# Turning attention probabilities by transposing DMAs in place of TensorE transposes, in a four-mixer hybrid block

## The chip, the cores and the metric

The kernel runs on one core of a Trainium2 chip. A core has five engines with a program each: TensorE (PE) multiplies matrices into PSUM banks, VectorE (DVE) and ScalarE (ACT) work on SBUF and PSUM, GpSimd (POOL) on SBUF, and SyncE (SP) issues DMAs. Each engine works its own list of instructions in order and waits on semaphores. The metric is the device time of one execution in microseconds; lower is better.

## The reference

One layer of a decoder over 2048 tokens of width 1024. The input is normalised and projected; four groups of heads mix over the sequence; the result is gated, projected by `w_out`, normalised and added to the input. What matters of it, cut:

```python
h = _rmsnorm(x, pre_norm[l])
(a_q, a_k, a_v, sb_q, sb_k, sb_v, f_q, f_k, f_v, f_logit, m_q, gate) = jnp.split(h @ w_in[l], COL_SPLITS, axis=-1)
# differential: softmax(q0 k0 + bias) - lam * softmax(q1 k1 + bias), times v, then a head norm
p = jax.nn.softmax(logits, axis=-1)
a = p[:, 0] - lam * p[:, 1]
# stick-breaking: a = sigmoid(z) * product of sigmoid(-z) over the keys between
log_rest = jnp.where(strict, jax.nn.log_sigmoid(-z), 0.0)
tail = lax.cumsum(log_rest, axis=3, reverse=True) - log_rest
a = jnp.where(strict, jnp.exp(jax.nn.log_sigmoid(z) + tail), 0.0)
# forgetting: softmax(q k + c_q - c_k), c the running sum of log sigmoid gates
# memory: softmax(q km) vm over 256 memory tokens
y = y * jax.nn.silu(gate)
x = x + _rmsnorm(y @ w_out[l], post_norm[l])
```

## The kernel before

The kernel has three parts, one block of instructions each. The first (the head) normalises and turns x and mem, and makes the memory keys and values and the forget sums. The second (the middle) does everything from the projections to the gated y. The third is the output projection.

The middle works through 16 units: for each of four lanes (128 columns of every group) a memory, a stick-breaking, a differential and a forgetting unit. A unit has 16 steps, one for each tile of 128 queries. In a step the scores of a row of keys are made in chunks of at most 512 columns, one PSUM bank each, three banks in all (`scores`, line 1079). Operands are fp16 pairs, a high and a low half, and a product is three matmuls (high times high, high times low, low times high), so that it keeps nearly fp32 accuracy.

What happens to a chunk:

- Soft kinds (memory, differential, forgetting): VectorE copies the bank to an fp32 row in SBUF and takes its maximum (`soft_chunk`), ScalarE makes the exponential (line 1240). In a differential unit VectorE then combines both rows (`combine`).
- Stick-breaking: ScalarE makes sigmoid(-z) into a slot of `temps` (line 1201) and sigmoid(z) into the row (line 1203); the bank is free then. VectorE runs a product along the slot (`stick_chunk`, a scan) and multiplies it into the row (`weigh`).
- Then each piece, at most four tiles of 128 keys, is turned: TensorE transposes it in fp32 against the identity into one of two PSUM banks `turned` (`turn`, line 1134), ScalarE copies it as fp16 to the high half of `turned_halves` (line 1227), VectorE subtracts that from the bank for the low half (line 1448). TensorE multiplies both halves with the values into the one bank `mixed` (`mix`, line 1149), and ScalarE takes it out (line 1233).

There are 864 such pieces: in each lane 16 in the memory unit, 80 in stick-breaking, 40 in differential, 80 in forgetting.

Beside this TensorE does the jobs, the projections of the next unit's Q, K and V and of the gates (`part`, line 1074). They need nothing from the running unit and stand between its work. Their results are brought into the `planes` and from there by DMA into `stack`, where the score matmuls read them (`stacks`, lines 1016 to 1029); these copies wait until the last scores of the unit before are done.

The order of the instructions on each engine is written by a planner in the kernel (`Plan.run`). It keeps a queue for each kind of task, gives each task a duration and a lag, and at each turn issues the task that can start first; among those of one engine that can start at the same time the lowest number of `RANK` wins. `AHEAD`, `SLACK` and `LATE` say how far the projections are to be ahead of the attention. The waits in the program, not the planned times, keep the data right.

## Time and profile before

| | us |
|---|---|
| median of 3 runs (2929.01 to 2929.6) | 2929.37 |
| the profiled execution, its own time | 2925.86 |
| its span | 2924.0 |
| TensorE busy (weight loads apart) | 2737.3 |
| VectorE busy | 2154.1 |
| ScalarE busy | 1616.5 |
| GpSimd busy | 194.4 |

Busy time is the union of the instructions' spans on an engine. Matmuls are pipelined, and their ends are modelled, so that the mean of one is longer than its share of the busy time. "Idle before" is the time that an engine stood still ahead of a group, with what ended it. TensorE's clock (PEclk) is a share of its full speed, 2.4 GHz.

### The profile page before, as it was taken

What the parts mean: (1) busy time and instruction counts of PE and PEld (TensorE: products, weight loads), DVE (VectorE), ACT (ScalarE), POOL (GpSimd) and SP (SyncE); (2) the same over time, 40 slices, a digit from 0 to 9 for tenths busy, and PEclk for the clock granted to TensorE, in tenths of its full rate; (3) what the DMA queues carried; (4) which work ended last, traced back from release to release, by engine and by line L of the source; (5) the groups of instructions that cost most, each with busy time, mean ns of one, the idle gap of its engine ahead of it and who ended that gap; (6) DMA issues with size and microseconds to landing.
All of it is one profiled execution on the core that took longest, in us unless ns stands there. A gap on an engine that the chain in (4) does not pass through costs nothing. (4 is left out here: it accounts for less than half of the span.)

```text
span 2924.0 us, 76171 instructions
## 1 busy us (share of the span) xinstructions
PE 2737.3 (94%) x29978; PEld 1970.3 (67%) x29978; DVE 2154.1 (74%) x5964; ACT 1616.5 (55%) x4307; POOL 194.4 (7%) x854
## 2 busy tenths in 40 slices
PE   2679999999999999999999999999999999779998
PEld 2357777778777777787777777877777778534443
DVE  6555898888768988888689988786898888631111
ACT  4324665557756655677566556675665566631212
POOL 0000001310000013100000131000001310000000
PEclk6789999999999999999999999999999999989999
DMA  3232102020111120211111202102112010153331
GB/s 105 69 92 59 44 20 71 16 58 24 43 43 40 29 71 16 54 27 33 53 38 31 71 16 51 29 28 58 38 30 69 10 38 24 48 183 102 107 110 43
DMA packets 178810, 152.82 MB, mean 52 GB/s; under 512 B 10988, under 2 KB 169588, under 8 KB 178444
## 3 DMA queue, kind: packets, MB, share of 16 engines
q1 hardware_dynamic: 178008, 146.90, 18.3%
q8 instruction: 240, 3.93, 0.6%
q0 software_dynamic: 448, 1.05, 0.1%
q14 instruction: 114, 0.93, 0.1%
HBM read 79.66 MB, written 26.84 MB: 36 GB/s over the span
## 5 line engine op out<-in xcount | busy, mean ns | idle before, releaser
L1074 PE MATMUL job<-wt,big 128*128 128x128 f16 x10752 | 684.3, 219 | 15.3 <-DVE gate_s L1354 13.7
L1074 PE MATMUL job<-big,wt 128*128 128x512 f16 x2688 | 667.6, 380 | 6.0 <-PEq L621 4.1
L1074 PEld LDWEIGHTS job<-wt,big 128*128 128x128 f16 x10752 | 632.1, 98 | 59.6 <-DVE gate_s L1354 21.5
L1448 DVE TENSOR_TENSOR turned_halves<-turned,turned_halves 128x512 f16<-128x512 f32 (+3 forms) x864 | 490.1, 588 | 93.6 <-ACT turned_halves L1227 90.9
L1227 ACT CAST turned_halves<-turned 128x512 f16<-128x512 f32 (+3 forms) x864 | 426.2, 520 | 217.0 <-PE turned L1134 212.5
L1240 ACT ACTIVATE rows<-rows,neg_max 128x512 f32<-128x512 f32 (+3 forms) x704 | 449.2, 642 | 87.4 <-DVE neg_max L1320 85.9
L1134 PE MATMUL turned<-ident,rows 128*128 128x128 f32 x2848 | 437.6, 276 | 11.1 <-DVE turned_halves L1448 6.5
L1120 PE MATMUL scores<-stack 128*128 128x512 f16 (+3 forms) x1600 | 425.5, 347 | 8.6 <-DMA stack<-planes 6.2
L1149 PE MATMUL mixed<-values,turned_halves 128*128 128x64 f16 (+1 forms) x8544 | 411.5, 199 | 5.2 <-issue 2.3
L1149 PEld LDWEIGHTS mixed<-values,turned_halves 128*128 128x128 f16 x8544 | 373.9, 98 | 59.1 <-DVE turned_halves L1448 17.8
L1074 PEld LDWEIGHTS job<-big,wt 128*128 128x128 f16 x2688 | 250.7, 98 | 237.1 <-issue 7.5
L1312 DVE TENSOR_SCALAR_CACHE_REDUCE rows<-scores 128x512 f32<-128x512 f32 (+3 forms) x704 | 398.4, 586 | 15.7 <-PE scores L1120 13.9
L1134 PEld LDWEIGHTS turned<-ident,rows 128*128 128x128 f32 x2848 | 318.2, 141 | 96.6 <-issue 21.4
L1293 DVE TENSOR_TENSOR_SCAN temps<-temps 128x512 f32<-128x512 f32 (+3 forms) x320 | 346.1, 1092 | 28.8 <-ACT temps L1201 23.2
L1201 ACT ACTIVATE temps<-scores 128x512 f32<-128x512 f32 (+3 forms) x320 | 176.7, 552 | 144.1 <-DVE rows L1306 120.8
L1120 PEld LDWEIGHTS scores<-stack 128*128 128x128 f16 x1600 | 141.2, 98 | 94.7 <-ACT rows L1203 10.0
L1306 DVE TENSOR_TENSOR rows<-rows,temps 128x512 f32<-128x512 f32 (+4 forms) x320 | 187.7, 602 | 0.9
L1203 ACT ACTIVATE rows<-scores 128x512 f32<-128x512 f32 (+3 forms) x320 | 177.4, 554 | 0.0
L1566 DVE TENSOR_TENSOR sc<-sc 128x1 f32<-128x1 f32 x16 | 2.5, 159 | 207.2 <-ACT job L1547 207.2
L1533 PE MATMUL scores<-big,rows 128*128 128x512 f16 x672 | 148.3, 383 | 5.3 <-DVE stack L1582 5.3
L1533 PE MATMUL turned<-big,rows 128*128 128x512 f16 x672 | 146.2, 379 | 0.0
L1233 ACT ACTIVATE o_copy<-mixed 128x128 f32<-128x128 f32 x256 | 72.1, 282 | 133.3 <-PE mixed L1149 93.9
(147 smaller groups left out, 2666.1 us busy)
## 6 DMA issues: line engine op xcount, KB each, us to landing
stack<-planes SPq DMA_DIRECT2D x160, 192.0 KB
ws<-w_in SPq DMA_DIRECT2D x56, 512.0 KB, 4.0
y_halves<-y_out_halves SPq DMA_DIRECT2D x64, 256.0 KB, 2.5
rows<-y_halves SPq DMA_DIRECT2D x16, 1024.0 KB, 7.9
rows<-x SPq DMA_DIRECT2D x16, 512.0 KB, 3.6
ws<-w_out SPq DMA_DIRECT2D x16, 512.0 KB, 3.9
stack<-x SPq DMA_DIRECT2D x16, 512.0 KB, 4.7
out<-stack SPq DMA_DIRECT2D x16, 512.0 KB, 2.9
```

The costliest lines, as they stand in the source:

```text
L1074: last = nc.tensor.matmul(dst, lhs, rhs, start=(k0 == 0 and q == 0), stop=(k1 == KT and q == len(pairs) - 1))
L1120: last = nc.tensor.matmul(bank[:, at:at + width], lhs, rhs, start=(q == 0), stop=(q == len(parts) - 1), skip_group_check=True)
L1134: last = nc.tensor.transpose(t_bank[tau % T_BANKS][:, k * P:(k + 1) * P], row(g, m)[:, (k0 + k) * P:(k0 + k + 1) * P], ident[:, :])
L1149: last = nc.tensor.matmul(o_bank[:, m * HEAD_DIM:m * HEAD_DIM + wide], turned[:, tau % PT_RING, a, k * P:(k + 1) * P], v[:, k0 + k, b, m * ...
L1203: nc.scalar.activation(row(g, m)[:, c:c + w], s_bank[n % S_BANKS][:, 0:w], ACT.Sigmoid) \
L1227: nc.scalar.copy(turned[:, tau % PT_RING, 0, 0:w], t_bank[tau % T_BANKS][:, 0:w]) \
L1240: nc.scalar.activation(mine, mine, ACT.Exp, bias=neg_max[:, r:r + 1], accum_out=z_part[:, r, c // BANK:c // BANK + 1]) \
L1293: nc.vector.tensor_tensor_scan(out=u[:, ::-1], data0=u[:, ::-1], data1=u[:, ::-1], initial=1.0 if first else temps[:, after:after + 1], op ...
L1306: nc.vector.tensor_tensor(mine, mine, temps[:, after:after + keys], ALU.mult) \
L1312: nc.vector.tensor_scalar(row(g, m)[:, c:c + w], s_bank[n % S_BANKS][:, 0:w], 1.0, -3.0e38, ALU.mult, ALU.max, accum_out=mx[:, r, c // BAN ...
L1448: nc.vector.tensor_tensor(turned[:, tau % PT_RING, 1, 0:w], t_bank[tau % T_BANKS][:, 0:w], turned[:, tau % PT_RING, 0, 0:w], ALU.subtract) \
L1533: last = nc.tensor.matmul(out_banks[i % 2][n][:, :], y[:, a, k, (i % 2) * P:(i % 2 + 1) * P], wo[:, b, k, n * BANK:(n + 1) * BANK], start= ...
```

## The change

The turn leaves TensorE. The piece is split before it is turned, not after: ScalarE copies the fp32 row as fp16 into a ring of four split buffers (`hi`), GpSimd subtracts it from the row for the low half (`lo`), and SP issues a transposing DMA that turns both halves into a ring of five buffers (`turn`), from which TensorE mixes. The PSUM banks of the turns go to a fourth score bank and a second mixing bank.

In stick-breaking the second sigmoid is made in place, in the score bank; `weigh` reads the bank and writes the row, and so the bank is free only after `weigh`. Its last column, which `weigh` leaves out, gets a sigmoid of one column (`stick_edge`). The scan takes its unused second input from the bank. Rows are now a ring of eleven chunks of 512 columns, freed by the split or by `combine`. Eight columns of sums and maxima are kept where four were. The planner's ranks, its costs and the numbers for the projections are others.

```diff
 RANK = {
-    "pe": {"turn": 0.51, "gate": 4.65, "y": 5.37, "mix": 5.92, "score": 6.18, "project": 6.81},
+    "pe": {"gate": -0.56896, "mix": -0.51359, "y": 1.56608, "score": 1.91373, "project": 3.21672},
...
-AHEAD = {0: 0.93, 1: 0.52, 2: 0.14, 3: 0.14}
-SLACK, LATE = 1.04, 4.77
-S_BANKS, T_BANKS, J_BANKS, PT_RING, ROWS = 3, 2, 2, 4, 4
+AHEAD = {0: 0.26397, 1: 0.48317, 2: 0.57988, 3: 0.81771}
+SLACK, LATE = 1.84466, 7.23605
+DVE_LOW = {"mem": 0, "stick": 0, "diff": 0, "forget": 0}
+S_BANKS, J_BANKS, O_BANKS, PT_RING, SPLIT_RING, ROW_RING, ROWS = 4, 2, 2, 5, 4, 11, 8
...
+                    if op == "turn":
+                        tau, m, k0, tiles = args[1]
+                        split_done(sp, tau)
+                        if tau >= PT_RING:
+                            sp.wait_ge(pv_done, tau - PT_RING + 1)
+                        sp.dma_start_transpose(
+                            turned[tau % PT_RING][:, 0:2 * tiles * P].rearrange("p (k q) -> p k q", q=P),
+                            split[tau % SPLIT_RING][:, 0:2 * tiles * P]).then_inc(turned_in[tau % PT_RING], 16)
...
-                            pe.wait_ge(stick_beta, plan.stick_at[q] + 1)
+                            pe.wait_ge(weighed, plan.stick_at[q] + 1)
...
-                def turn(g, tau, m, k0, tiles):
...
-                    for k in range(tiles):
-                        last = nc.tensor.transpose(t_bank[tau % T_BANKS][:, k * P:(k + 1) * P],
-                                                   row(g, m)[:, (k0 + k) * P:(k0 + k + 1) * P], ident[:, :])
-                    last.then_inc(t_full, 1)
...
-                    if first and g:
-                        pe.wait_ge(o_copied, g)
-                    pe.wait_ge(t_free, tau + 1)
+                    if first and g >= O_BANKS:
+                        pe.wait_ge(o_copied, g - O_BANKS + 1)
+                    turned_landed(pe, tau)
...
-                    nc.scalar.activation(row(g, m)[:, c:c + w], s_bank[n % S_BANKS][:, 0:w], ACT.Sigmoid) \
-                        .then_inc(stick_beta, 1)
+                    z = s_bank[n % S_BANKS][:, 0:w]
+                    if c + w == (plan.steps[g][1] + 1) * P:
+                        row_free(act, n)
+                        nc.scalar.activation(scored(n, w - 1, w), z[:, w - 1:w], ACT.Sigmoid).then_inc(stick_edge, 1)
+
+                def stick_weights(g, n, m, c, w):
+
+                    act.wait_ge(stick_u, plan.stick_at[n] + 1)
+                    act.wait_ge(stick_edge, plan.edges[n])
+                    z = s_bank[n % S_BANKS][:, 0:w]
+                    nc.scalar.activation(z, z, ACT.Sigmoid).then_inc(stick_beta, 1)
...
+                        if tau >= SPLIT_RING:
+                            turned_landed(act, tau - SPLIT_RING)
+                        nc.scalar.copy(halves_of(tau, 0, w), scored(n, 0, w)).then_inc(split_hi, 1)
...
+                    if op == "lo":
+                        tau, m, k0, tiles = args[1]
+                        w = tiles * P
+                        pool.wait_ge(split_hi, tau + 1)
+                        nc.gpsimd.tensor_tensor(halves_of(tau, 1, w), scored(plan.chunk_at(g, m, k0), 0, w),
+                                                halves_of(tau, 0, w), ALU.subtract).then_inc(low_pool, 1)
...
-                    nc.vector.tensor_tensor(mine, mine, temps[:, after:after + keys], ALU.mult) \
+                    nc.vector.tensor_tensor(mine, s_bank[n % S_BANKS][:, 0:keys], temps[:, after:after + keys], ALU.mult) \
                         .then_inc(weighed, 1)
```

With `DVE_LOW` at zero every low half is GpSimd's.

How the instructions of TensorE stand, in the last step of the second stick-breaking unit. Before, L1120 are scores, L1134 the turns, L1149 the mixes and L1074 jobs:

```order
L1074 MATMUL job<-big,wt 128x512 x2
L1134 MATMUL turned<-ident,rows 128x128 [waits t_free,weighed]
L1134 MATMUL turned<-ident,rows 128x128 x3
L1074 MATMUL job<-big,wt 128x512 x3
L1120 MATMUL scores<-stack 128x512 [waits stick_beta]
L1120 MATMUL scores<-stack 128x512
L1134 MATMUL turned<-ident,rows 128x128 [waits t_free,weighed]
L1134 MATMUL turned<-ident,rows 128x128 x2
```

After, in the same step, L1182 are scores, L1197 the mixes and L1136 jobs:

```order
L1182 MATMUL scores<-stack 128x512 [waits weighed]
L1182 MATMUL scores<-stack 128x512
L1197 MATMUL mixed<-values,rows 128x64 [waits turned_in0]
L1197 MATMUL mixed<-values,rows 128x64 x8
L1136 MATMUL job<-big,wt 128x512 [waits j_free]
L1136 MATMUL job<-big,wt 128x512 x5
L1197 MATMUL mixed<-values,rows 128x64 [waits turned_in1]
L1197 MATMUL mixed<-values,rows 128x64 x11
L1136 MATMUL job<-big,wt 128x512 x6
L1182 MATMUL scores<-stack 128x512 [waits weighed]
```

The turns are gone, the scores wait for `weighed` in place of `stick_beta`, and the mixes wait for a DMA (`turned_in0` to `turned_in4`).

How SP's DMAs stand at the end of the first stick-breaking unit, where the operands of the differential unit are brought in. Before, L1024 and L1029 are these operand copies, L988 a load of weights, L1042 a store of y:

```order
L1042 DMA y_halves<-y_out_halves 128x2x512 [waits j_free]
L988 DMA ws<-w_in 128x8x128 [waits w_ready]
L1024 DMA stack<-planes 64x3x512 [waits j_free,s_full]
L1029 DMA stack<-planes 64x3x512
L1024 DMA stack<-planes 64x3x512
L1029 DMA stack<-planes 64x3x512
L1024 DMA stack<-planes 64x3x512 [waits j_free,s_full]
```

After, L1095 are the turns, L1078 and L1083 the operand copies and L1042 a load of weights:

```order
L1095 DMA_TRANSPOSE rows<-rows 128x6x128 [waits pv_done,low_pool]
L1095 DMA_TRANSPOSE rows<-rows 128x8x128 [waits pv_done,low_pool]
L1042 DMA ws<-w_in 128x8x128 [waits w_ready]
L1095 DMA_TRANSPOSE rows<-rows 128x8x128 [waits pv_done,low_pool] x4
L1078 DMA stack<-planes 64x3x512 [waits j_free,s_full]
L1083 DMA stack<-planes 64x3x512
L1078 DMA stack<-planes 64x3x512
L1083 DMA stack<-planes 64x3x512
L1078 DMA stack<-planes 64x3x512 [waits j_free,s_full]
```

The copies and the loads of weights now stand behind turns, each of which waits for GpSimd (`low_pool`) and for a mix five pieces before (`pv_done`).

## Rows read from the trace of the kernel before

**Rows 1.** The page's first part: busy time, share of the span, instructions
```profile
PE 2737.3 (94%) x29978; PEld 1970.3 (67%) x29978; DVE 2154.1 (74%) x5964; ACT 1616.5 (55%) x4307; POOL 194.4 (7%) x854
```

**Rows 2.** Three stretches: us, busy time of each engine, TensorE's clock, DMA share, GB/s
```profile
0.00:180.00 180.00, 85.59 (x531) 60.16 (x532) 107.51 (x193) 64.09 (x116) 8.68 (x22) 0.70 0.32 90
180.00:2549.00 2369.00, 2312.96 (x27912) 1758.78 (x27910) 1970.57 (x5627) 1467.46 (x4048) 185.69 (x832) 1.00 0.15 40
2549.00:2924.00 375.00, 338.77 (x1536) 151.40 (x1536) 76.04 (x144) 84.96 (x144) 0.00 (x0) 0.95 0.39 114
```

**Rows 3.** Two windows of the second round, stick-breaking and forgetting
```profile
896.00:1042.40 146.40, 145.76 (x1780) 107.46 (x1778) 144.41 (x236) 99.85 (x236) 0.00 (x0) 1.00 0.12 31
1237.60:1360.00 122.40, 122.06 (x1639) 96.35 (x1638) 101.25 (x350) 86.45 (x257) 2.48 (x13) 1.00 0.09 24
```

**Rows 4.** Costliest groups: line, engine, shapes, busy us, mean ns, idle before
```profile
L1448 DVE TENSOR_TENSOR turned_halves<-turned,turned_halves 128x512 f16<-128x512 f32 (+3 forms) x864 | 490.1, 588 | 93.6 <-ACT turned_halves L1227 90.9
...
L1134 PE MATMUL turned<-ident,rows 128*128 128x128 f32 x2848 | 437.6, 276 | 11.1 <-DVE turned_halves L1448 6.5
...
L1566 DVE TENSOR_TENSOR sc<-sc 128x1 f32<-128x1 f32 x16 | 2.5, 159 | 207.2 <-ACT job L1547 207.2
```

**Rows 5.** The same two windows, the transposes of line 1134 alone
```profile
896.00:1042.40 146.40, 31.86 (x206) 22.93 (x206) 1.00 0.12 31
1237.60:1360.00 122.40, 33.67 (x225) 25.27 (x225) 1.00 0.09 24
```

**Rows 6.** The same two windows, the subtractions of line 1448 alone
```profile
896.00:1042.40 146.40, 34.70 (x59) 1.00 0.12 31
1237.60:1360.00 122.40, 38.62 (x68) 1.00 0.09 24
```

**Rows 7.** Groups by shape, columns as in rows 4
```profile
L1120 PE MATMUL scores<-stack 128*128 128x512 f16 x1120 | 335.7, 379 | 0.2
L1227 ACT CAST turned_halves<-turned 128x512 f16<-128x512 f32 x560 | 323.0, 596 | 150.6 <-PE turned L1134 148.9 <-PE mixed L1149 1.0
L1240 ACT ACTIVATE rows<-rows,neg_max 128x512 f32<-128x512 f32 x448 | 320.8, 719 | 53.3 <-DVE neg_max L1320 53.0
...
L1293 DVE TENSOR_TENSOR_SCAN temps<-temps 128x512 f32<-128x512 f32 x224 | 283.7, 1269 | 22.1 <-ACT temps L1201 16.5
...
L1203 ACT ACTIVATE rows<-scores 128x512 f32<-128x512 f32 x224 | 138.9, 620 | 0.0
...
L1306 DVE TENSOR_TENSOR rows<-rows,temps 128x512 f32<-128x512 f32 x192 | 129.8, 682 | 0.0
...
L1194 ACT ACTIVATE values<-job 128x128 f16<-128x128 f32 x192 | 54.0, 283 | 101.3 <-PE job L1074 99.7
```

**Rows 8.** GpSimd's groups by shape
```profile
L1260 POOL TENSOR_TENSOR root<-root_i,root 128x1 f32<-128x1 f32 x64 | 17.3, 270 | 5.3
...
L669 POOL MEMSET ident<- 128x128 f32 x1 | 0.2, 205 | 0.3 <-POOLq L1599 0.3
...
L1599 POOL MEMSET const-bfloat16-1.0<- 128x1 bf16 x1 | 0.1, 101 | 0.0
```

**Rows 9.** One window at the start of the second forgetting unit
```profile
1213.20:1237.60 24.40, 23.61 (x272) 18.69 (x271) 20.34 (x61) 15.07 (x41) 2.82 (x15) 1.00 0.54 126
```

**Rows 10.** SP's DMA issues in order of time: start us, us, line
```profile
1377.16 0.38 SPq L988 DMA_DIRECT2D ws<-w_in  x1
...
2387.64 0.79 SPq L1019 DMA_DIRECT2D stack<-c_scale  x1
...
2402.84 0.61 SPq L1027 DMA_DIRECT2D temps<-planes  x1
```

**Rows 11.** The DMA queues, and issues with KB and median us to landing
```profile
q1 hardware_dynamic: 178008, 146.90, 18.3%
...
y_halves<-y_out_halves SPq DMA_DIRECT2D x64, 256.0 KB, 2.5
```

190 lines of the change are left out of this document (114 added, 76 removed).

## The prediction

> **What bounds the kernel now.** I read the page's totals first, then its span cut into three stretches, then windows inside the long stretch, and last the groups by shape. The totals put TensorE at 94% of the span and VectorE at 74% [rows 1]; the others follow from the stretches. The three stretches show where that is earned: in the 2369 us of attention and projections TensorE is busy 2312.96 us, so it stands still for 56 us, while VectorE has 398 us and ScalarE 902 us to spare; the granted clock there is 1.00 [rows 2]. The head (180 us) and the output projection (375 us) are hardly touched by the change. The middle is four rounds over the lanes, with four units each: memory, stick-breaking, differential, forgetting. So TensorE bounds the middle, with one reservation: in the stick-breaking window VectorE is busy 144.41 of 146.40 us and TensorE 145.76, so both stand at the limit there, while in the forgetting window VectorE has 21 us left [rows 3].
>
> **Part 1: the turns leave TensorE.** Before, each piece of probabilities is turned by fp32 transposes against the identity: 2848 of them in 864 pieces, 437.6 us of TensorE together, 154 ns each [rows 4]. Nothing takes their place on TensorE, as the order of its instructions shows (scores, mixes and project parts alone). All lie in the middle, where TensorE is the bound: -438 us. In the two windows it is -31.86 and -33.67 us [rows 5]: stick-breaking would go to 146.4 - 31.9 = 114.5, forgetting to 122.4 - 33.7 = 88.7 us.
>
> **Part 2: the split leaves VectorE.** The subtraction that makes the low half, 490.1 us in 864 instructions [rows 4], goes to GpSimd. In the stick-breaking window that takes 34.70 us from VectorE [rows 6]: 144.4 - 34.7 = 109.7, below TensorE's 113.9. Without it part 1 would win nothing there. In forgetting 101.3 - 38.6 = 62.7 us. So VectorE doesn't become the bound.
>
> **Part 3: ScalarE.** The high half is now copied from SBUF, not from a PSUM bank. The PSUM copy of 512 columns takes 596 ns, an exp of 512 columns from SBUF 719 [rows 7]; so between 0 and 0.12 us more a piece, and I take 0.05. The second sigmoid writes to the bank instead of SBUF: 620 ns now [rows 7], and no nearer row for a PSUM target, so I leave it. New is a one-column sigmoid for each row of keys, 128 in all; a ScalarE instruction of 128 columns takes 283 ns [rows 7], so at most 36 us over the kernel, and I take 0.25 us each. In the stick-breaking window ScalarE goes from 99.85 to about 99.9 + 59 x 0.05 + 24 x 0.25 = 109 us (24 of a unit's 32 such columns fall in the window). Below 114, but now three engines stand within 5 us of each other there.
>
> **Part 4: GpSimd.** It has 864 subtractions of 422 columns on average (2848 x 128 / 864) and one per piece on a path of its own. No row shows it working at such a width. From below: its memset goes from 101 ns at one column to 205 at 128 [rows 8], 0.8 ns a column, and 0.1 + 422 x 0.0008 = 0.44 us is the least a piece can cost by that. From above: its one-column two-input operation takes up to 270 ns [rows 8] where VectorE takes 159, 1.7 times; times VectorE's 588 ns for the very subtraction [rows 4] that is 1.0 us. I take 0.85. The forgetting window has 68 pieces, and 88.7 / 68 = 1.30 us is what a piece may cost before it decides: GpSimd stays under it.
> The Trainium skill (GPSIMD Engine Reference, Elementwise, side-by-side cycle accounting) has a two-input add at 4497 ns for 2048 fp32 columns against VectorE's 2293, a ratio of 1.96. By it a piece would be 0.588 x 1.96 = 1.15 us, an estimate; no row here shows it, and the sum would be the same, but the margin to the limit would shrink from 0.45 to 0.15 us.
>
> **Part 5: the transposing DMAs.** 864 of them on SP's queue, each with the two halves of a piece, 211 KB on average, 186.6 MB in all. The trace has no transposing DMA. Lower end: the queue moved 126 GB/s at a share of 0.54 while it copied stacks from SBUF to SBUF [rows 9], so 233 GB/s when busy and 0.93 us for 216,000 bytes; with 0.38 us to issue a plain one [rows 10], 1.31 us if the two don't overlap. Upper end: 178,008 packets took 18.3% of 16 engines' 2924 us [rows 11], 48 ns each; if the queue had to move a transposed row of 128 halves (256 bytes) as a packet, a piece is 844 packets and 2.5 us. I take 1.31, since rows of the same kind of copy are nearest. 864 x 1.31 = 1132 us beside a middle of some 2000: hidden on the whole. The landing counts too, because the copy of the high half waits until the piece four before has landed. A store of 256 KB lands after 2.5 us [rows 11]: (0.5 copy + 0.85 + 0.3 of waits, my guess, + 2.5) / 4 = 1.04 us a piece; at twice that landing, 5.0 us, it is 1.66.
> The Trainium skill (DMA: Bandwidth & Descriptors, Latency and other measured facts) gives the transposing DMA 261 GB/s, up to 350-400 when contiguous. By it 216,000 bytes take 0.83 us, an estimate, and the sum stays; no run here has shown it yet.
>
> **Part 6: what is queued behind.** SP issues in order. The operand copies of the next unit, 0.60 us or more each, 21 of them in one go from 2387.64 to 2403.4 us [rows 10], now stand between turns, and a turn in front of them holds them until its piece is split and a ring slot is free. TensorE then waits at the mix, and everything behind it. Before, that queue held only loads, operand copies and stores, none of which waited for a piece. The score bank is also held longer, until the weights are formed: 0.76 for two score matmuls + 0.62 + 0.62 + 1.27 + 0.68 [rows 7] = 3.95 us, over four banks 1.0 us a chunk, where VectorE needs 1.95 (scan and weigh): hidden. Two mixing banks take away waits of TensorE for the copy of the mixed rows, a part of its 56 us of standing still [rows 2]: taken as nothing, since others are as near behind.
>
> **The sum.** -438 for the turns. Given back: in stick-breaking three engines at 109 to 114 of 114.5 us won't interleave without gaps; I put 5% of 114 on the window, which holds 59 of the unit's 80 pieces, 8 us a unit, 32 us. In forgetting SP needs 1.31 a piece where 1.30 is there, plus 28 operand copies at 0.65 (18 us) in a unit; half of that shows, 9 us a unit, 36 us. Together +68. Span: 2924 - 438 + 68 = 2554. The profiled execution took 2925.86, 1.9 us more than its span, and the median of the runs is 3.5 us above that: **2559 us**, 12.6% less.
>
> **The rivals.**
> A (60%): the above, with a range of its own from 2490 (nothing given back) to 2640 (twice as much and the same again at the units' borders).
> B (25%): a piece costs 2.0 us on the way from ScalarE's copy over GpSimd and SP to the landing, and that path sets the pace of the units rich in pieces. A unit has 80 pieces; by the windows [rows 3, 5] stick-breaking now lasts 146.4 x 80/59 = 198 us and would go to 155, forgetting 144 and would go to 104. At 2.0 us both become 160: +5 and +56, four times, +244, so 2924 - 438 + 244 and 5 from the span to the median, 2735. For it: the ring of four and the in-order queue; against it: project parts that TensorE can do meanwhile, and the prices above. It decides from 1.30 us a piece in forgetting.
> C (10%), slower: the turn is bound by the DMA engines at small packets, 2.5 us: 864 x 2.5 = 2160, plus 15% of the middle that they are busy now (355 us) [rows 2], makes a middle of 2515 instead of 2369, 2924 + 146 = 3070, so 3075. The point where it turns slower is (2369 - 355) / 864 = 2.33 us a piece. For it: 48 ns a packet; against it: the instruction moves blocks, and it would have to cost 1.8 times what I take.
> D (4%): TensorE, with more waits, falls to the lower of its levels for part of the time. In the head its granted clock is 0.70 with TensorE busy 86 of 180 us [rows 2]. If a tenth of the new middle ran at 1.2 GHz, half of 2.4, that is +200 us: 2760.
> E (1%): no difference, if each stretch already hangs on something other than TensorE. The 99% in the stick-breaking window speak against it, unless VectorE's 144.4 was the cause and its relief is used up by new waits.
>
> **Chances.** This kernel's median can tell changes from 0.2% on. A, B and D are faster: 0.89. C is slower: 0.10. Same: 0.01. The range from 2490 to 2780 takes in A, B and D and leaves out C and the tails, some 15%.
>
> **What would show it.** Right: no fp32 transposes in the middle, TensorE's total near 2300 us, clock at 1.00, the middle 1930 to 2030 us, VectorE's total near 1660, GpSimd some 900 to 1000 us, a subtraction at 0.6 to 1.1 us, and SP's transposing issues at 1.3 us or less apart where they are dense. Wrong for A and right for B: TensorE waiting for turned pieces by more than 100 us in all, in the forgetting units above all, and ScalarE's high copies waiting for landings. Right for C: the DMA engines' share above 0.8 in the middle and TensorE idle everywhere. For D: a granted clock under 1.00 in the middle. If the stick-breaking unit doesn't shrink while the others do, part 2 or 3 was wrong.

## The result, and the profile after

The changed kernel takes 2954.59 us (median of 4 runs, 2950.5 to 2957.67) where the kernel before, on the same chip, takes 2929.45. The ratio is 1.0084 [1.0071, 1.0096]: slower by 0.84%, 25 us. The forecast was 2559 us. Both the sign and the range were wrong.

The page's totals, the queue that SP feeds, and the row of the turning DMAs (count, median us to landing):

```profile
PE 2505.8 (85%) x27130; PEld 1694.4 (57%) x27130; DVE 1842.2 (62%) x5100; ACT 1650.4 (56%) x4435; POOL 1059.7 (36%) x1718
...
q1 hardware_dynamic: 934744, 333.66, 57.0%
...
rows<-rows SPq DMA_TRANSPOSE x864, 3.2
```

Against [rows 1, 11]: TensorE works 231.5 us less, VectorE 312 less, GpSimd 865 more, and the queue has 756,736 packets more. The same three stretches as in [rows 2] (stretch, its length, PE, PEld, DVE, ACT, POOL busy, TensorE's clock, DMA share, GB/s):

```profile
0.00:180.00 180.00, 86.95 (x530) 62.23 (x530) 107.54 (x193) 64.03 (x115) 8.72 (x22) 0.68 0.32 90
180.00:2574.00 2394.00, 2081.15 (x25064) 1481.35 (x25064) 1658.58 (x4763) 1501.37 (x4176) 1051.00 (x1696) 0.96 0.63 117
2574.00:2948.00 374.00, 337.74 (x1536) 150.82 (x1536) 76.07 (x144) 84.99 (x144) 0.00 (x0) 0.96 0.38 114
```

Head and tail are unchanged, and the middle is 25 us longer. Two numbers carry the case. TensorE's busy time in the middle fell by 231.8 us (2312.96 to 2081.15), not by 438. And TensorE stands still for 312.9 us there, where it stood 56: 256.8 more. The clock of the middle is 0.96 instead of 1.00, and the DMA engines' share 0.63 instead of 0.15.

What TensorE stands still for, by the waits of the middle (who waited for what: us, times, longest):

```profile
POOL rows L1332 <- ACT rows L1290: 979.7, 502, 33.5
...
PEld mixed L1197 <- DMA rows<-rows: 241.4, 168, 14.6
PE mixed L1197 <- DMA rows<-rows: 193.7, 112, 14.4
...
ACT rows L1290 <- DMA rows<-rows: 114.9, 104, 5.9
...
DVE rows L1381 <- POOL rows L1332: 88.8, 105, 2.5
```

PEld is TensorE's loading of weights, which runs ahead of its multiplications (PE). Both wait in the same gaps, so these two rows are not added: the mixes stand some 200 to 240 us for turned pieces. Cut at the last mix of each unit, and summed over the four rounds, the middle divides like this (us; the last column is the part of the 193.7 us):

| units | length before, after | TensorE stands still before, after | mixes wait for turned pieces |
|---|---|---|---|
| memory | 263, 235 | 20, 26 | 1 |
| stick-breaking | 880, 793 | 13, 78 | 62 |
| differential | 678, 780 | 8, 102 | 63 |
| forgetting | 541, 578 | 9, 99 | 67 |

The jobs can stand in another unit after the change, so the lengths alone don't compare like with like. The standing still does: it is spread over three kinds of unit, and most of the differential units' waits is one hole of 11 to 15 us at the end of each. GpSimd's first row shows that it is no bottleneck on the whole; it waits 980 us for ScalarE's high halves. VectorE's wait for GpSimd is for a free row of the ring of eleven. Two of the places where it happens show in windows of 60 us, at the border from a differential to a forgetting unit and inside that forgetting unit. After:

```profile
1800.00:1860.00 60.00, 43.52 (x495) 32.24 (x494) 33.17 (x108) 26.26 (x73) 24.47 (x54) 0.89 0.52 111
1920.00:1980.00 60.00, 51.26 (x650) 34.28 (x649) 33.47 (x106) 45.63 (x118) 36.82 (x35) 0.97 0.95 169
```

Before, TensorE was busy 58.95 and 59.30 us of such windows. At the border every engine idles and the DMA engines are half empty: something is held, not slow. Inside the unit the DMA engines are full at 0.95, while TensorE, VectorE and ScalarE are all idle part of the time.

The border in SP's list, in order of time (start us, us, line):

```profile
1805.87 2.62 SPq L1095 DMA_TRANSPOSE rows<-rows  x2
1808.59 0.83 SPq L1073 DMA_DIRECT2D stack<-c_scale  x1
...
1823.54 0.61 SPq L1081 DMA_DIRECT2D temps<-planes  x1
1824.25 2.65 SPq L1095 DMA_TRANSPOSE rows<-rows  x2
```

For 15.7 us, 21 operand copies in a row, no piece is turned. The prediction's Part 6 looked at the reverse order (copies behind turns); turns behind copies hold TensorE too, because the mix that waits stands in TensorE's own list ahead of all its other work:

```profile
1811.02 2.17 PE L1136 MATMUL job<-wt,big 128*128 128x128 f16 x36
1827.60 1.46 PE L1197 MATMUL mixed<-values,rows 128*128 128x128 f16 x12 [14.41 <-DMA rows<-rows]
```

The price of the transposing DMA on SP (duration in ns, min/median/max, then the first and last start in us):

```profile
L1095 SPq DMA_TRANSPOSE rows<-rows x864: 1167/1254/3761, 200.3 to 2562.5; - x173
```

and of the two operations ahead of it, by shape (busy us, mean ns of one, idle before):

```profile
L1332 POOL TENSOR_TENSOR rows<-rows 128x512 f16<-128x512 f32 x560 | 655.5, 1180 | 584.5 <-ACT rows L1290 581.5
...
L1290 ACT CAST rows<-rows 128x512 f16<-128x512 f32 x560 | 344.2, 620 | 208.6 <-DMA rows<-rows 94.1 <-DVE rows L1414 92.7 <-DVE rows L1374 18.5
```

A turn takes SP 1.25 us to issue (median), nearly whatever its width (1.20 us at 128 columns and 1.27 at 512). The DMA engines need 1.33 us for the mean piece: (57.0% of 2948.7 - 18.3% of 2924) / 864. The queue carries 216 KB more per piece in 876 packets, so about one packet per 256 bytes. Issue and transfer run beside each other: inside the forgetting unit turns of 512 columns follow at 1.38 us in a burst, where the DMA engines by their mean rate (163 GB/s) need 1.61 us for such a piece, an estimate, and the two in sequence would be 2.9. Over the whole of this unit a turn starts every 1.77 us.

VectorE shows something that the forecast didn't have. With its subtractions gone, its groups in the middle add up to 394 us less (2265 to 1871), though the subtractions alone were 498 of that: the small instructions that take two operands from SBUF became slower. One of them, before and after:

```profile
L1410 DVE SCALAR_TENSOR_TENSOR y_f<-o_copy,root,gate_s 128x128 f32<-128x128 f32 x64 | 22.1, 346 | 23.5 <-PE job L1074 12.1 <-POOL root L1262 11.2
...
L1478 DVE SCALAR_TENSOR_TENSOR y_f<-o_copy,root,gate_s 128x128 f32<-128x128 f32 x64 | 55.8, 872 | 28.7 <-POOL root L1324 25.4 <-PE job L1136 2.8
```

Of these 64, the 47 that overlap with a subtraction on GpSimd take 1061 ns on average, the other 17 take 350. VectorE's maxima, which read a PSUM bank, stay as they were (683 and 686 ns at 512 columns).

### The profile page after: what moved, and what is told of

Its sections match the earlier page's. It is cut to its first block and busy times, and to the rows that moved or that the text cites. A ratio compares the mean times of both kernels' runs of the same rounds, so it can differ in the third digit from the quotient of the medians.

```text
span 2948.7 us, 72476 instructions
## 1 busy us (share of the span) xinstructions
PE 2505.8 (85%) x27130; PEld 1694.4 (57%) x27130; DVE 1842.2 (62%) x5100; ACT 1650.4 (56%) x4435; POOL 1059.7 (36%) x1718
## 3 DMA queue, kind: packets, MB, share of 16 engines
q0 software_dynamic: 448, 1.05, 0.1%
## 5 line engine op out<-in xcount | busy, mean ns | idle before, releaser
L1332 POOL TENSOR_TENSOR rows<-rows 128x512 f16<-128x512 f32 (+3 forms) x864 | 858.3, 1006 | 983.4 <-ACT rows L1290 979.7
L1136 PE MATMUL job<-wt,big 128*128 128x128 f16 x10752 | 689.9, 222 | 14.5 <-DVE y_out_halves L1343 6.4
L1136 PE MATMUL job<-big,wt 128*128 128x512 f16 x2688 | 682.9, 386 | 20.3 <-DVE y_out_halves L1343 9.9
L1136 PEld LDWEIGHTS job<-wt,big 128*128 128x128 f16 x10752 | 639.9, 100 | 77.6 <-DVE y_out_halves L1343 16.1
L1197 PE MATMUL mixed<-values,rows 128*128 128x64 f16 (+1 forms) x8544 | 452.8, 203 | 225.7 <-DMA rows<-rows 193.7
L1290 ACT CAST rows<-rows 128x512 f16<-128x512 f32 (+3 forms) x864 | 462.9, 546 | 255.5 <-DMA rows<-rows 114.9
L1197 PEld LDWEIGHTS mixed<-values,rows 128*128 128x128 f16 x8544 | 391.2, 100 | 360.5 <-DMA rows<-rows 241.4
L1182 PE MATMUL scores<-stack 128*128 128x512 f16 (+3 forms) x1600 | 445.0, 354 | 32.4 <-DVE rows L1381 16.5
L1136 PEld LDWEIGHTS job<-big,wt 128*128 128x128 f16 x2688 | 246.9, 99 | 264.2 <-issue 34.1
L1361 DVE TENSOR_TENSOR_SCAN temps<-temps,scores 128x512 f32<-128x512 f32 (+3 forms) x320 | 347.5, 1089 | 31.4 <-ACT scores L1259 23.0
L1182 PEld LDWEIGHTS scores<-stack 128*128 128x128 f16 x1600 | 142.1, 101 | 123.8 <-DVE rows L1381 34.6
L1374 DVE TENSOR_TENSOR rows<-scores,temps 128x512 f32<-128x512 f32 (+4 forms) x320 | 187.6, 603 | 8.8 <-DVE temps L1361 0.9
L1599 PEld LDWEIGHTS scores<-big,rows 128*128 128x128 f16 x1008 | 99.0, 98 | 125.9 <-issue 8.2
L1259 ACT ACTIVATE scores<-scores 128x512 f32<-128x512 f32 (+3 forms) x320 | 167.1, 544 | 1.3
L1422 DVE SCALAR_TENSOR_TENSOR gate_s<-gate_t,job 128x128 f32<-128x128 f32 x256 | 72.8, 284 | 121.8 <-ACT gate_t L1276 119.4
L1302 ACT ACTIVATION_READ_ACCUMULATOR rows<-rows,neg_max 128x1 f32 x704 | 133.7, 190 | 0.0
```

The lines of the kernel that those rows point to most:

```text
L1136: last = nc.tensor.matmul(dst, lhs, rhs, start=(k0 == 0 and q == 0), stop=(k1 == KT and q == len(pairs) - 1))
L1182: last = nc.tensor.matmul(bank[:, at:at + width], lhs, rhs, start=(q == 0), stop=(q == len(parts) - 1), skip_group_check=True)
L1197: last = nc.tensor.matmul(o_bank[g % O_BANKS][:, m * HEAD_DIM:m * HEAD_DIM + wide], turned[tau % PT_RING][:, (a * tiles + k) * P:(a * tile ...
L1259: nc.scalar.activation(z, z, ACT.Sigmoid).then_inc(stick_beta, 1)
L1290: nc.scalar.copy(halves_of(tau, 0, w), scored(n, 0, w)).then_inc(split_hi, 1)
L1302: nc.scalar.activation(mine, mine, ACT.Exp, bias=neg_max[:, r:r + 1], accum_out=z_part[:, r, c // BANK:c // BANK + 1]) \
```

## The experiments

Each edit is shown against the kernel that is named with it. "Changed" is the kernel after the change. Ratios are to the kernel before, timed beside each run; that median lies between 2928.5 and 2931.2 us, so a difference in us between two runs can be off by some 3.

Few results fell where one of the two theories had them: the costs for SP, both cuts together, plain copies in the order of costs and width, and the new order. The run with costs and width lies in the ranges of both, and all others lie outside both.

### One transpose a piece in the kernel before

```diff
-                    for k in range(tiles):
+                    for k in range(1):
                         last = nc.tensor.transpose(t_bank[tau % T_BANKS][:, k * P:(k + 1) * P],
```

> The kernel before, with one transpose a piece instead of up to four: 864 in place of 2848; three quarters of the probabilities aren't turned and the mixes read what the bank held. Theory W (the turns were worth less than I took): the 437.6 us of their row overlapped with the matmuls around them, since the rows of TensorE add up to more than its busy time; a turn frees about 0.11 us at most, and in stick-breaking VectorE holds the pace: 1984 x 0.11 = 220 us at most, so 2710 to 2800. Rival (the prediction's own count, 154 ns each): 1984 x 0.154 = 305 us less, about 2625.

Measured: 2903.02 us, 0.991 [0.9896, 0.9925]. Its totals, and the two windows of [rows 3]:

```profile
PE 2625.3 (91%) x27994; PEld 1752.8 (60%) x27994; DVE 2149.2 (74%) x5964; ACT 1607.0 (55%) x4307; POOL 195.1 (7%) x854
```

```profile
896.00:1042.40 146.40, 138.57 (x1622) 89.27 (x1619) 144.37 (x234) 97.14 (x228) 0.00 (x0) 1.00 0.12 32
1237.60:1360.00 122.40, 114.36 (x1550) 79.78 (x1548) 104.63 (x350) 96.61 (x281) 0.00 (x0) 1.00 0.08 23
```

For the tiles that aren't turned, the mixes read what the bank held. 1984 transposes less take 112.0 us from TensorE's busy time (2737.3 to 2625.3), 56 ns each, not the 154 ns of [rows 4]. And of these 112 us only 26 reach the end. In the stick-breaking window VectorE now stands at 144.37 of 146.40 us while TensorE has 8 us left: VectorE sets the pace there.

### The low half for one tile only, in the kernel before; and both together

```diff
-                        nc.vector.tensor_tensor(turned[:, tau % PT_RING, 1, 0:w],
-                                                t_bank[tau % T_BANKS][:, 0:w],
-                                                turned[:, tau % PT_RING, 0, 0:w], ALU.subtract) \
+                        nc.vector.tensor_tensor(turned[:, tau % PT_RING, 1, 0:P],
+                                                t_bank[tau % T_BANKS][:, 0:P],
+                                                turned[:, tau % PT_RING, 0, 0:P], ALU.subtract) \
...
-                                turned[:, tau % PT_RING, a, k * P:(k + 1) * P],
+                                turned[:, tau % PT_RING, a, (1 - a) * k * P:(1 - a) * k * P + P],
```

> The kernel before, with the low half made for the first 128 columns of a piece alone, about 0.28 us in place of 0.59, so some 250 us less of VectorE; the mixes read that tile for all. Theory V (in the stick-breaking units VectorE was the bound, TensorE only looked busy, since 1984 fewer transposes gave 26 us): 40 to 100 us less, 2830 to 2890, though TensorE does all that it did. Theory P (TensorE was the bound): within 10 us of 2929.

> The kernel before with both cuts: one transpose a piece, and the low half of 128 columns. Theory V and W together (both engines stood at the limit, and one alone can't shorten the middle): more than the sum of the two alone, at least 60 us below the narrow low half alone, about 2750. Rival (a fixed order of waits holds the pace whatever the engines do): no more than the sum of the two, 26 us plus that of the narrow low half.

Measured: 2893.57 us, 0.9884 [0.9867, 0.99], for this edit alone; 2786.16 us, 0.9513 [0.9499, 0.9528], with the edit of the first experiment too. Alone they are worth 26 and 35 us, together 142. The stick-breaking window with the low half cut:

```profile
896.00:1042.40 146.40, 146.11 (x1848) 111.05 (x1846) 131.93 (x239) 103.55 (x239) 0.00 (x0) 1.00 0.14 37
```

Now VectorE has 14 us left and TensorE none. So in the kernel before both stand at the limit, and taking work from one alone gives little. The change relieves both, so its loss isn't there; but what was to be had from the whole change is of the order of 142 us, not 438 (these cuts leave a transpose and a tile of the subtraction for each piece, so it is an estimate). The pages' totals, with the low half cut and with both cuts, also warn of what a busy time is:

```profile
PE 2714.8 (94%) x29978; PEld 1977.0 (68%) x29978; DVE 1937.9 (67%) x5964; ACT 1622.1 (56%) x4307; POOL 194.2 (7%) x854
...
PE 2561.4 (92%) x27994; PEld 1757.0 (63%) x27994; DVE 1920.1 (69%) x5964; ACT 1599.1 (57%) x4307; POOL 194.2 (7%) x854
```

TensorE's busy time fell by 22.5 us with none of its instructions taken away, and by 175.9 us with the same 1984 gone that gave 112.0 alone. It moves with what the other engines do, and no single price of a transpose fits all three runs.

### Plain copies in place of the transposing DMAs, and half the bytes

Against the changed kernel, plain copies of the same bytes to the same place:

```diff
-                        sp.dma_start_transpose(
-                            turned[tau % PT_RING][:, 0:2 * tiles * P].rearrange("p (k q) -> p k q", q=P),
+                        sp.dma_start(
+                            turned[tau % PT_RING][:, 0:2 * tiles * P],
```

> The changed kernel with the same order, where each transposing DMA is a plain copy of the same bytes; the probabilities are not turned. Theory D (the transposing DMAs themselves hold TensorE up, by 1.25 us of issue each and by small packets): issue falls to about 0.4 us and the packets become 2 KB, so most of TensorE's 313 us of standing still goes, and its clock goes back to 1.00: 2650 to 2750 from 2954. Rival G (GpSimd's subtraction at 1.0 us or the ring of four is the bound, or the order is bad for other reasons): within 40 us of 2954.

Measured: 2826.96 us, 0.9651 [0.9636, 0.9665], 128 us less than the changed kernel. With only the high half turned (`0:tiles * P` in the DMA, and the mixes reading it for both halves):

> The changed kernel with only the high half turned: half the bytes and packets, as many issues; the mixes read the high half in place of the low one. It splits theory D. If the DMA engines' throughput holds (share 0.92 in the forgetting units): the share falls to about half of that and 100 us or more go, 2850 or less. If SP's issue in order holds: the issue stays at 1.25 us and less than 40 us go. If the issue time grows with the blocks, it falls to about 0.7 us and both go.

Measured: 2881.22 us, 0.9833 [0.9818, 0.9848], 73 us less. SP's queue on the page, first with plain copies:

```profile
q1 hardware_dynamic: 302424, 333.60, 37.4%
```

then with half the bytes transposed:

```profile
q1 hardware_dynamic: 570200, 240.34, 37.4%
```

By the same sum as above, per piece the DMA engines spend 0.6 us on the plain copy of 216 KB (144 packets) and 0.63 us on the transposed half of it (454 packets), against 1.33 us for the whole transposed: a transposed byte costs 2.2 times a copied one. The issue hardly depends on the size: 1209 ns (median) for half the bytes, 1254 for all, and 465 for the plain copy. So the transposed half costs the DMA engines as much as the plain copy, and differs from it mainly by its issue. That splits the 128 us, if the two parts add up: 73 for the time in the DMA engines, with the landing that comes with it (3.2 us fell to 2.4), and 54 for the issue on SP. Cut as in the table above, the plain copies shorten the forgetting units by 53 us in all, the stick-breaking ones by 38 and the differential ones by 24: it is not a matter of forgetting alone.

### The planner's costs for SP

The order of the changed kernel was planned with a stack of operand copies at 0.1 to 0.5 us on SP. The trace has seven copies of 0.6 us or more for a forgetting stack. With costs from the trace, all else as changed:

```diff
-                                    {"mem": 0.1, "forget": 0.5}.get(unit.kind, 0.3), 3.6))
+                                    {"mem": 0.65, "forget": 4.9}.get(unit.kind, 2.6), 3.6))
...
-            q["strip"].append((("strip", n), ("strip", n), [("w_lo", n - 2)] if n >= 2 else [], 0.1, 4.0))
+            q["strip"].append((("strip", n), ("strip", n), [("w_lo", n - 2)] if n >= 2 else [], 0.4, 4.0))
...
-        q["store"] = deque((("store", g), ("store", g), [("y_lo", g)], 0.1, 2.6)
+        q["store"] = deque((("store", g), ("store", g), [("y_lo", g)], 0.4, 2.6)
```

> The changed kernel with the planner's cost for the operand copies on SP as the trace has them (0.65, 2.6 and 4.9 us in place of 0.1, 0.3 and 0.5) and 0.4 in place of 0.1 us for loads and stores; all else the planner's. Theory Q (the copies at the units' borders hold turns that the order thought free): the gap at the border of differential and forgetting, where TensorE is busy 43 of 60 us, fills by a part, 20 to 60 us less, 2900 to 2935. Rival: the order can't help, since the copies have to be issued there anyway: within 10 us of 2954.

Measured: 2902.89 us, 0.9899 [0.988, 0.9917]: 52 us less than the changed kernel, and less than before. Next, the turn's cost grows with its width as well, `max(1.27, 0.1 + w * 0.0028)` for 1.27:

> The changed kernel with the copies' real costs on SP as in the run before this one (2903 us), and the turn booked by its width, 0.1 + 0.0028 us a column but at least 1.27 (1.53 at 512 columns), in place of 1.27 for all. Theory D/Q: in the forgetting units, where the DMA engines' share is 0.92, the order now leaves room for the transfers, and TensorE's waits for turned pieces fall from 295 us: 2870 to 2900. Rival (the order is right to a few us once the copies are): 2895 to 2910.

Measured: 2896.87 us, 0.9893 [0.9878, 0.9907]. The intervals of the two runs overlap, so the width shows no gain of its own. The stretch at the border, 1810 to 1840 us, in the changed kernel:

```profile
1810.00:1840.00 30.00, 15.35 (x154) 11.40 (x154) 10.27 (x38) 9.99 (x30) 3.97 (x14) 0.77 0.50 114
```

and with costs and width, where the same copies are issued earlier:

```profile
1770.00:1800.00 30.00, 28.46 (x325) 20.71 (x322) 20.66 (x63) 16.68 (x45) 11.61 (x17) 1.00 0.63 138
```

The hole is gone, and with it the clock of 0.77. The waits of the mixes for turned pieces fell as well, from 241.4 us in all and 14.6 at the longest, first with the costs and then with costs and width:

```profile
PEld mixed L1197 <- DMA rows<-rows: 172.0, 183, 3.6
...
PEld mixed L1197 <- DMA rows<-rows: 108.2, 123, 2.8
```

What the order changed there isn't SP's list: 21 operand copies still stand in a row, for 16.4 us. It is TensorE's list. The two engines beside each other, with costs and width:

```profile
1775.16 0.82 SPq L1073 DMA_DIRECT2D stack<-c_scale  x1
...
1779.71 4.70 PE L1136 MATMUL job<-big,wt 128*128 128x512 f16 x21
...
1787.06 5.34 PE L1136 MATMUL job<-big,wt 128*128 128x512 f16 x24
...
1791.52 4.00 SPq L1095 DMA_TRANSPOSE rows<-rows  x3
...
1794.83 0.84 PE L1197 MATMUL mixed<-values,rows 128*128 128x128 f16 x12 [0.26 <-DMA rows<-rows]
```

While SP issues the copies, TensorE has jobs and the first scores of the next unit, and the mix comes when its piece has landed. So the hole at the borders was the work of the order: with seven copies planned at 0.5 us, the mix was put in front of the jobs, as if its turn were near.

### The operand copies from GpSimd's queue

Taken from the kernel with the new costs, the stacks' copies issued by GpSimd instead of SP:

```diff
-    "pool": {"root": 0.00000, "lo": 1.00000},
-    "sp": {"stacks": 0.00000, "pairs": 0.50000, "turn": 0.80000, "strip": 1.00000, "sums": 2.00000,
+    "pool": {"stacks": -1.00000, "root": 0.00000, "lo": 1.00000},
+    "sp": {"pairs": 0.50000, "turn": 0.80000, "strip": 1.00000, "sums": 2.00000,
```

> The kernel with the copies' real costs, and the operand copies issued from GpSimd's queue in place of SP's, so that no turn stands behind them on SP. Theory Q (SP's order at the borders): the borders shrink again, 2860 to 2890. Rival: the low halves now stand behind the copies on GpSimd, or the DMA engines themselves are full there, and nothing is won: 2895 to 2930.

Measured: 2953.11 us, 1.0086 [1.0066, 1.0107], 50 us more than with the same copies on SP. GpSimd's waits (us, times, longest):

```profile
POOL stack L1050 <- DVE planes L1345: 81.2, 7, 19.6
POOL stack L1045 <- PE scores L1182: 37.6, 3, 14.1
```

The copies wait for the last scores and the last planes of the unit, up to 19.6 us, and now the low halves stand behind them in GpSimd's list. The mixes' waits for turned pieces rose from 172.0 to 207.7 us. The likely reading is that the hold moved to another engine. But no run parts these waits from two other differences: the 256 copies take about 0.6 us of GpSimd each, some 150 us in all, and they travel in another queue, where a stack copy lands after 4.9 us.

### Low halves of the forgetting units back on VectorE

From "costs and width", `DVE_LOW` at 1 for forgetting:

> The kernel with real costs and widths (2897 us), with the low halves of the forgetting units made by VectorE, which idles there nearly half the time, in place of GpSimd: 0.6 us a piece in place of 1.2. Theory G (GpSimd is a part of the limit in forgetting): 20 to 60 us less. Theory D (the transposing DMAs are the limit there, share 0.9): within 15 us of 2897.

Measured: 2928.63 us, 0.9994 [0.9982, 1.0005], 32 us more. The subtraction on VectorE and on GpSimd in that run:

```profile
L1332 POOL TENSOR_TENSOR rows<-rows 128x512 f16<-128x512 f32 x336 | 395.6, 1189 | 486.0 <-ACT rows L1290 485.2
...
L1514 DVE TENSOR_TENSOR rows<-rows 128x512 f16<-128x512 f32 x224 | 151.9, 688 | 34.2 <-ACT rows L1290 32.7
```

It is 1.7 times as fast on VectorE, and yet the kernel is slower, against both expectations. So a faster low half brought nothing by itself; whether GpSimd's pace costs time in forgetting stays open, since the move also loads VectorE (its busy time rose by 155 us). Why it costs 32 us isn't settled: VectorE's 34.2 us before the subtractions, waiting for ScalarE with its own list held, are of that size, but no run took them away. The run does show what slowed VectorE's small instructions. The gating of y in the forgetting units, with costs and width and then in this run:

```profile
L1473 DVE SCALAR_TENSOR_TENSOR y_f<-o_copy,rz,gate_s 128x64 f32<-128x64 f32 x128 | 51.9, 446 | 2.2
...
L1473 DVE SCALAR_TENSOR_TENSOR y_f<-o_copy,rz,gate_s 128x64 f32<-128x64 f32 x128 | 30.8, 282 | 2.2
```

With GpSimd's subtractions gone from these units they take 282 ns again, as in the kernel before.

### A new order for the same program

From the trace-based costs (the width cost at 0.0030 a column, ScalarE's high half at 0.06 + w * 0.00083, TensorE's row at 1.05), the ranks and the numbers for the projections were chosen anew by the planner's own planned end. The program's instructions are those of the changed kernel:

```diff
-    "sp": {"stacks": 0.00000, "pairs": 0.50000, "turn": 0.80000, "strip": 1.00000, "sums": 2.00000,
-            "store": 3.00000, "near_in": 4.00000},
+    "sp": {"stacks": 11.533, "pairs": 1.122, "turn": -23.07, "strip": 1.042, "sums": 3.888, "store": 23.896, "near_in": 6.819},
...
-SLACK, LATE = 1.84466, 7.23605
+SLACK, LATE = 2.7013, 47.8238
```

> The changed kernel with the planner's costs set from the trace (operand copies, loads and stores on SP, turns 0.1 + 0.0030 a column, the high copy 0.06 + 0.00083 a column, TensorE's rate at the granted clock) and ranks, AHEAD, SLACK and LATE chosen anew for them. Theory O (what the change has left to win is in the order): 2820 to 2880, the fastest of the full kernels. Rival (the transfers in the forgetting units set a floor that no order moves): 2885 to 2905.

Measured: 2847.09 us, 0.9713 [0.9699, 0.9728]. It is the fastest complete kernel of this study, 2.9% below before and 107.5 us below the changed one. Its middle:

```profile
180.00:2471.00 2291.00, 2053.78 (x25064) 1458.88 (x25064) 1653.45 (x4763) 1498.27 (x4176) 1054.45 (x1696) 0.98 0.67 123
```

TensorE stands still for 237 us in place of 313, and the clock is 0.98. To be fair to the kernel before, it got the same treatment: SP's costs and TensorE's row from the trace, ranks and numbers chosen anew.

> The kernel before, its planner given the real costs of SP's DMAs and ranks, AHEAD, SLACK and LATE chosen anew for them, in the same way as for the replanned changed kernel (2847 us). It asks whether that kernel won by its program or only by a better order. Theory P (the old program is at its limit in every stick-breaking and forgetting unit, so an order can give it little): 2915 to 2932. Rival (the order was worth as much there): 2820 to 2880.

Measured: 2902.09 us, 0.9904 [0.9889, 0.9919], so 28 us from a better order alone. That is outside both ranges, nearer to the first. Like against like, the change of the program is worth 2902.1 - 2847.1 = 55 us, 1.9%, with the best order found for each; how near either is to its best isn't known.

### Plain copies again, in the better orders

The plain copies of the second experiment, in the order of "costs and width" and in the new order:

> The order of the run with real costs and widths (2897 us), with plain copies in place of the transposing DMAs; the probabilities are not turned. With the changed kernel's own order the same swap took 128 us off (2955 to 2827). Theory D (in both orders the transposing DMAs cost TensorE time of their own, and the order only took away the holds at the borders): again 60 to 100 us less, 2800 to 2840. Rival (the better order has already hidden the transposing DMAs): 2870 or more.

> The replanned changed kernel (2847 us) with plain copies in place of the transposing DMAs; the probabilities are not turned. In the two orders before, the swap took off 128 and 78 us. Theory H (an order that knows their length hides more and more of them): 20 to 60 us less, 2790 to 2825. Rival (a fixed price of the transposing DMAs of some 80 us): 2770 or less.

Measured: 2819.0 us, 0.9615 [0.9599, 0.9631], 78 us less than with transposing DMAs; and 2777.02 us, 0.9478 [0.9464, 0.9492], 70 us less, which lies between the two forecasts: the better orders hide about half of the 128 us, and the last step from 78 to 70 is hardly more than the noise. The middle of the second:

```profile
180.00:2400.00 2220.00, 2035.90 (x25064) 1452.54 (x25062) 1656.44 (x4763) 1486.31 (x4176) 1052.05 (x1696) 0.99 0.40 126
```

and what TensorE still waits for there:

```profile
PEld scores L1179 <- DVE rows L1378: 55.4, 63, 2.9
PEld job L1133 <- DVE gate_s L1419: 46.2, 64, 2.0
...
PEld mixed L1194 <- DMA rows<-rows: 36.3, 39, 3.8
```

With the DMA cheap and the order better, TensorE still stands for 184 us, mostly for VectorE, which is busy 1656 of 2220 us. This kernel and the one with both cuts in the kernel before (2786) meet within 9 us. They cut different amounts in different orders, so how closely they meet is chance; but both put what the relief of the two engines can bring near 150 us.

### The banks

From the changed kernel, one mixing bank (`O_BANKS = 1`), and three score banks (`S_BANKS = 3`), the bank left over being kept by a name of its own:

> The changed kernel with one mixing bank in place of two, its order planned for that. I took the second bank as worth nothing: within 12 us of 2955. Rival (with landings of 3.2 us on the way a mix can't wait for the copy of the last one as well): 30 us or more slower, 2985 or above.

> The changed kernel with three score banks in place of four, its order planned for that. The prediction held a bank for 3.95 us a chunk; over three banks 1.3 us, and VectorE needs 1.95: within 15 us of 2955. Rival (the bank held until the weights are formed now starves the stick-breaking units): 40 us or more slower.

Measured: 2980.4 us, 1.017 [1.0155, 1.0185], and 2980.9 us, 1.0178 [1.0161, 1.0194]. Each bank is worth 26 us in the changed kernel, between the two forecasts in both cases. With one mixing bank TensorE waits for ScalarE to take the mixed rows out:

```profile
PEld mixed L1197 <- ACT o_copy L1295: 59.2, 70, 2.3
```

a wait of 8.0 us (weight loads) in the changed kernel. With three score banks it is VectorE that stands: its maximum's copy waits 145.7 us for scores instead of 57.3.

## Why the prediction was wrong

The forecast for the middle was -438 of busy time and +68 given back, -370. Measured: -231.8 of busy time and +256.8 of standing still, +25. Of the 395 us between them, 206 are the first term and 189 the second.

**Part 1 (-438) is the first step that failed.** The direction was right: no fp32 transposes are left, and TensorE's work fell. The size was not. I took a group's busy time from [rows 4] as what the engine would be spared. Such spans overlap with those of the groups beside them, since matmuls are pipelined and their ends modelled. The first experiment measured 56 ns for a transpose in place of 154; for 2848 that would be 160 us, and the whole change took 232. Whether those that open a piece are dearer, or the busy time fell for other reasons as it did in the run with the low half cut, isn't settled. A warning stood in the trace before any run: the busy times of TensorE's groups in that stretch add up to 2961 us, where the engine's union is 2313 [rows 2].

**"TensorE bounds the middle" was half of it.** Removing three quarters of the transposes alone gives 26 us, most of VectorE's subtraction alone 35, both 142. I had seen the two at 145.76 and 144.41 of 146.40 us [rows 3] and had used it for Part 2 alone. I should have capped the gain there: two engines that stand at 99% in turn, each held by the other's order, don't shrink by the work that is taken from them. A part of the gain goes into waits for each other, as the 184 us of the kernel with plain copies and the new order show.

**Part 2** was too large as well. The forecast had VectorE's total near 1660 us; it came to 1842.2. It fell by 312 us, not by 490. That the middle alone measures 1659 is chance. Two things went into the difference: VectorE's groups overlap too (2265 us of groups in 1971 of busy time), and its small instructions became slower beside GpSimd's subtraction, by 104 us in sum. What Part 2 needed, VectorE below TensorE, came all the same. **Part 3** held within its bounds: 620 ns against 596 for the high copy, and 0.19 us for the edge. **Part 4** took 0.85 us and measured 1.006, the upper bound. At 512 columns it is 1180 ns against VectorE's 688 for the same operands, the ratio of 1.7 by which I had the bound. The ratio of 1.96 in the Trainium skill (GPSIMD Engine Reference, Elementwise, side-by-side cycle accounting) gave 1.15 for the mean piece, an estimate; this case measured less. What Part 4 left out is what the subtraction does to VectorE.

**Part 5** had the right sum, 1.31 us, for two wrong reasons that met: the issue alone is 1.25 (I had 0.38), and the DMA engines need 1.33 beside it (I had 0.93). They overlap and don't add up. 216 KB in 1.33 us are 163 GB/s. The Trainium skill gives a transposing DMA 261 GB/s and 350 to 400 when contiguous (DMA: Bandwidth & Descriptors, Latency and other measured facts); the two differ, and the measurement decides. What failed was "hidden on the whole". 1132 us in 2394 are hidden as an average, but not where pieces come in a row: in a forgetting unit the share is 0.95, and the mixes of the stick-breaking units wait for turned pieces nearly as long (62 us and 67). In three orders the transposing DMAs cost 128, 78 and 70 us over plain copies.

**Part 6 and the +68 are the second step that failed.** The place was right (SP's list at the unit borders, and forgetting), the size was not: 36 us for SP in forgetting, 32 in stick-breaking and nothing at the end of the differential units. Measured, TensorE stands still 90 us more in forgetting, 65 in stick-breaking and 94 in the differential units. SP's true costs in the planner take off 52 us, a better order overall 107.5. I had read where the operand copies stand in the list, but not compared the planner's cost for them (0.1 to 0.5 us) with the trace's (0.65 to 4.9). "Taken as nothing" for the two banks was wrong too: 26 us each.

**The rivals.** B's place and its signs came (TensorE waits for turned pieces by over 100 us, ScalarE's high copies for landings, 114.9 us), but not "in the forgetting units above all", and its price, 2735, came almost from forgetting alone. C's sign in the DMA share came in forgetting only. D's did in part: 0.96 where I named 1.00. If the clock was low in as large a share of TensorE's busy time as of the whole middle, that is 2081 x 0.04 = 83 us more than at full clock, an estimate. The holes came first: at the border TensorE is busy half the time, at 0.77. The stick-breaking units did get shorter (880 to 793 us in sum), so the sign against Part 2 and 3 stayed away. A's upper end doesn't follow from its own words: twice the 68 gives 2627, and 68 more for the borders 2695, not 2640; the measured time lies above them all. What part of the 25 us is clock isn't settled, since no run kept the holes and not the clock.

**The sum, as the runs close it.** 2777 us with cheap DMAs in a good order, 152 below before; 70 for transposing DMAs; 107.5 for the order that came with the change: 2954.6. These are differences between the runs' own times and add up by construction; taken in another order the shares are others (128 for the transposing DMAs in the order that came with the change). Not settled are the price of the sigmoid in place, which no run took alone, that of VectorE's low halves in forgetting, and how much of the whole the slower VectorE costs beside GpSimd.

## What to carry to other kernels

- Before a group's busy time becomes a gain, add up the groups of its engine; where they exceed its total, expect a smaller gain. And where two engines are full in the same window, expect little from relieving one; relieving both gives more than the two gains alone (142 us against 26 and 35 here), but far less than the work that their groups seem to hold.
- When a queue that only carried loads gets work that others wait for, its order becomes part of the critical path: give the planner the durations of the trace before judging the change, and plan the kernel before anew as well. Here that decided between 0.8% slower and 2.9% faster.
- A resource's average says little: 1.3 us a piece is hidden as a mean over the kernel, and not where pieces come one behind the other.
- When work moves to another engine, look at what the old one still does beside it: here VectorE's small instructions took up to three times as long.

## What the runs showed of the hardware

- A transposing DMA from SBUF to SBUF, 2-byte elements, up to 128 x 1024: 1.21 us on SP (median) for a mean of 108 KB and 1.25 us for 216 KB, 0.63 and 1.33 us of the 16 DMA engines, landing after 2.4 and 3.2 us. A plain copy of the 216 KB: 0.465 us, 0.6 us, and 2.3 us at 256 KB.
- It moves in packets of about 256 bytes, at 1.5 ns each over 16 engines (24 ns of one), half of the 48 ns a packet by which rival C was priced.
- An operand copy issued by GpSimd that waits holds the whole of GpSimd's list, 19.6 us at the longest.
- A VectorE instruction that reads both operands from SBUF takes longer while GpSimd subtracts in SBUF: `y_f` at 128x128 took 1061 ns where the two overlap and 350 where they don't.
- TensorE's busy time isn't the sum of fixed prices: without 1984 transposes it fell by 112.0 us, with VectorE relieved as well by 175.9.
